# Decoder trunk with grouped experts, one core: expert gate and up weights laid out with eight consecutive rows per partition

## The reference, cut to what matters

```
def grouped_moe(x, w_router, b_router, w_gate, w_up, w_down):
    gates = shared_group_router(xt, w_router, b_router)      # two non-zero gates per token
    for e in range(N_EXPERTS):                               # 16
        h = silu(xt @ w_gate[e]) * (xt @ w_up[e])            # [512, 1024] @ [1024, 512], twice
        out = out + gates[:, e:e + 1] * (h @ w_down[e])      # [512, 512] @ [512, 1024]
```

## Time and profile before

| | |
|---|---|
| median of 3 runs | 888.58 us (884.96 to 889.7) |
| profiled execution | 889.47 us, span 888.0 us from first to last instruction |
| mean granted TensorE clock | 0.981 |
| PE busy, share of the span | 851.6 us, 96% |
| PEld | 707.0 us, 80% |
| DVE | 574.0 us, 65% |
| ACT | 465.0 us, 52% |
| POOL | 76.0 us, 9% |
| DMA | 195.87 MB in 168097 packets, mean 221 GB/s |

### The profile page before, as it was taken

The page is one execution under the profiler, slowest core; times in us unless marked ns, Lnnn a source line. Parts: engine busy times, 40 slices in busy tenths (PEclk is TensorE's granted clock), DMA queues, the critical chain, the costliest instruction groups (busy, mean ns, idle before and its releaser), DMA issues.

```text
span 888.0 us, 12634 instructions
## 1 busy us (share of the span) xinstructions
PE 851.6 (96%) x4090; PEld 707.0 (80%) x4091; DVE 574.0 (65%) x623; ACT 465.0 (52%) x482; POOL 76.0 (9%) x137
## 2 busy tenths in 40 slices
PE   9999999979999999999999999799999999999993
PEld 8788788858888888888888987688888888888751
DVE  4887444334448874423555698479898988888727
ACT  4555542423566653422325641477888787778610
POOL 1000000500000000000000002200101010010040
PEclk9999999989999999999999999799999999999997
DMA  7465555963333345433319915799999999999753
GB/s 203 171 182 165 173 191 193 256 239 91 95 94 95 95 114 170 119 100 112 95 52 325 293 41 214 262 338 379 380 372 382 382 381 371 380 381 382 245 185 122
DMA packets 168097, 195.87 MB, mean 221 GB/s; under 512 B 7998, under 2 KB 106918, under 8 KB 168070
## 3 DMA queue, kind: packets, MB, share of 16 engines
q1 hardware_dynamic: 154374, 157.69, 53.4%
q0 software_dynamic: 10624, 32.57, 10.7%
q10 hardware_dynamic: 3072, 5.24, 1.6%
HBM read 164.94 MB, written 30.54 MB: 220 GB/s over the span
## 4 chain that ended last, share of the span: by engine, by line
PE 72%; DMA 11%; DVE 9%; ACT 3%; issue 3%; POOL 1%; ACTq 0%; DVEq 0%; SPq 0%; POOLq 0%
PE psA L585 7%; PE psA L587 7%; PE psA L586 7%; DMA est<-in_w_exp_down_dram 6%; PE psB L585 6%; PE psB L587 6%; PE psB L586 6%; PE psA L756 4%; PE psA L758 4%; PE psA L757 4%; DVE elo L1334 2%; DMA wst<-in_w_out_dram 2%; PE psB L777 2%; PE psB L778 2%; PE psB L779 2%
## 5 line engine op out<-in xcount | busy, mean ns | idle before, releaser
L1334 DVE TENSOR_TENSOR elo<-est,ehi 128x2048 fp32r<-128x2048 f32 x94 | 211.5, 2288 | 37.3 <-ACT ehi L1005 32.0
L1005 ACT ACTIVATE ehi<-est 128x2048 fp32r<-128x2048 f32 x92 | 173.5, 1913 | 38.8 <-DMA est<-in_w_exp_down_dram 18.4
L1136 DVE TENSOR_TENSOR wlo<-wst,whi 128x1024 fp32r<-128x1024 f32 (+1 forms) x78 | 97.5, 1250 | 97.8 <-ACT whi L852 96.7
L852 ACT ACTIVATE whi<-wst 128x1024 fp32r<-128x1024 f32 (+1 forms) x78 | 83.9, 1076 | 92.5 <-PE psA L587 36.4
L756 PE MATMUL psA<-ehi,xe_hi 128*128 128x512 f32 x256 | 102.2, 399 | 1.9 <-DVE xe_lo L1527 1.8
L758 PE MATMUL psA<-ehi,xe_lo 128*128 128x512 f32 x256 | 100.5, 393 | 0.0
L757 PE MATMUL psA<-elo,xe_hi 128*128 128x512 f32 x256 | 100.5, 393 | 0.0
L585 PE MATMUL psB<-xT_hi,whi 128*128 128x512 f32 x208 | 80.9, 389 | 0.0
L586 PE MATMUL psB<-xT_lo,whi 128*128 128x512 f32 x208 | 80.9, 389 | 0.0
L587 PE MATMUL psB<-xT_hi,wlo 128*128 128x512 f32 x208 | 80.9, 389 | 0.0
L756 PEld LDWEIGHTS psA<-ehi,xe_hi 128*128 128x128 f32 x256 | 48.6, 190 | 12.8 <-DVE xe_lo L1527 3.1
(11 more groups left out here) (277 smaller groups left out, 1634.7 us busy)
## 6 DMA issues: line engine op xcount, KB each, us to landing
est<-in_w_exp_gate_dram SPq DMA_DIRECT2D x32, 1024.0 KB, 12.3
est<-in_w_exp_up_dram SPq DMA_DIRECT2D x32, 1024.0 KB, 10.8
est<-in_w_exp_down_dram SPq DMA_DIRECT2D x32, 1024.0 KB, 11.9
wst<-in_w_in_dram SPq DMA_DIRECT2D x60, 512.0 KB, 4.0
xs<-zero POOLq DMA_DIRECT2D x23, 512.0 KB, 2.9
wst<-in_w_out_dram SPq DMA_DIRECT2D x16, 512.0 KB, 6.4
wst<-in_w_branch_r_dram SPq DMA_DIRECT2D x8, 640.0 KB, 4.3
ys<-yb ACTq DMA_DIRECT2D x32, 160.0 KB, 5.1
```

What stands on the lines that cost most here:

```text
L852: A(whi[p][:, 0:K, :], wst[p][:, 0:K, :], ACT.Copy).then_inc(w_hi, 1)
L1005: A(ehi[s][:], est[s][:], ACT.Copy).then_inc(gu_hi if s < 4 else d_hi, 1)
L1136: V.tensor_tensor(wlo[p][:, 0:K, :], wst[p][:, 0:K, :], whi[p][:, 0:K, :], ALU.subtract).then_inc(w_lo, 1)
L1334: V.tensor_tensor(elo[s][:], est[s][:], ehi[s][:], ALU.subtract).then_inc(gu_lo if s < 4 else d_lo, 1)
```

## The change

Two things change together, in three lines.

- `load_expert` reads gate and up weights with the row index p*8 + k: partition p now holds the eight consecutive rows 8p to 8p+7, the first four in one piece and the last four in the other. So the part of a piece that goes to one partition is 8 KB without a gap in DRAM, and without a gap in the buffer. Down weights are loaded as before.
- The tokens' channels have to be grouped alike: piece k of the transpose is no longer columns 128k to 128k+127 of `xe` but every eighth column, k, k+8, k+16 and so on. Now the stationary operand of L744 and L788 is read with a step of 8 floats (32 bytes). What is written to PSUM, `xe_hi`, `xe_lo`, and all matmuls behind it keep their shapes, their number and their order. No instruction is added or removed, and no wait.

```
             if s < 4:
-                src = w.rearrange("(k p) n -> p k n", p=P)[:, 4 * (s % 2):4 * (s % 2) + 4, :]
+                src = w.rearrange("(p k) n -> p k n", p=P)[:, 4 * (s % 2):4 * (s % 2) + 4, :]
...
                 for k in range(KD):
                     mm = pe.transpose(psC[0][:, k // 4, (k % 4) * P:(k % 4 + 1) * P],
-                                      xe[:, k * P:(k + 1) * P], ident[:])
+                                      xe[:].rearrange("p (c k) -> p k c", k=KD)[:, k, :], ident[:])
...
                     mm = pe.matmul(psC[0][:, k // 4, (k % 4) * P:(k % 4 + 1) * P],
-                                   x1[:, t, k * P:(k + 1) * P], block0[:, t, :],
+                                   x1[:, t, :].rearrange("p (c k) -> p k c", k=KD)[:, k, :], block0[:, t, :],
                                    start=(t == 0), stop=(t == TT - 1))
```

## The result

Over 20 runs of each, the changed kernel takes 889.38 us (median) and the kernel before 886.66: the ratio is 1.0029, with a 95% interval of 1.0019 to 1.0040. It is slower by 0.3%, or 2.7 us, inside the 0.5% that I had called no change, and far from the 901.5 us that I held likeliest. The time lies in my range only because the range had been stretched to the free step.

A forecast was written before the change was run, and what follows sets the result against it. PE was taken to bound the expert stage, transfers right behind. 889.47 - 0.6 (loads) + 13.5 (strided operand: 11.5 + 2.0) = 902.4 us profiled, 901.5 as median; range 885.5 to 906, stretched to include the free step.

The forecast's parts named there:

- the free step: Rival: strided stationary loads in transposes and first block cost nothing, leaving only the loads' relief, 888.0 us median; chance 0.27.
- The packet line: Gate and up loads: 38 ns per KB plus 10 ns fixed per packet, so 8 KB pieces save 1.0 us per expert.
- What it brings the end: -0.6 us: Relieved loads: 0.4 us won at the last expert and 0.2 us in the output projection; bounds 0 to -1.5 us.
- `xe` lands 1.1 us later and stays covered: Expert stage: token rows queue behind longer packets, landing after 7.5 instead of 6.4 us, at no cost.
- The price of a strided load: 0.216 us instead of 0.109: TensorE's 128-column fp32 stationary loads in L744 and L788: a 32-byte step adds 0.107 us each.
- The road by VectorE's 1.84 ns an element: Price of a strided TensorE load taken from VectorE's 16-byte-step write: 0.236 us for 128 elements.
- What sets the pace of the transposes: `rows_t`: loading 128 fp32 weights sets the pace, so any slowing of the read is paid in full.
- The term of 11.5 us: Blocks 2 to 15: 14 times eight slower transpose loads in `rows_t`, 0.75 to 0.86 us per block.
- The first block: 2.0 us: L788's 64 strided loads add 6.8 us; after the covered wait and the clock, +1.2 to +2.8 us remain.
- the cover of 3.4 us: Before block 1: PE's wait for `xe` hides this much of L788's 6.8 us, so `rows_t(1)` starts 3.4 us later.
- the clock's gift: `gate_up(1)`: with a shorter wait before it, half clock need not follow, giving back up to 2.2 us.
- the two variants of the forecast, 1.2 and 2.8: First block's net cost: +1.2 us if half clock stays away behind it, +2.8 us if it returns; 2.0 taken.

The follow-up runs named there:

- e6: Kernel before with the eight transposes of `rows_t` replaced by plain fp32 products with the identity, no step: 898.43 us beside 885.11, one execution each.
- e7: Changed kernel with expert 0 in the old layout, L788 unstrided, and plain fp32 products reading `xe` at 32 bytes instead of the transposes: 927.07 us, one execution.
- e1: Kernel before with only the gate and up loads changed to 8 KB pieces, channels wrongly paired: 884.10 us, ratio 0.9977.
- e8: Repeat of e1, only the gate and up loads changed against the kernel before: 884.93 us against 886.80, ratio 0.9977.
- e3: Kernel before with only the transposes of `rows_t` reading `xe` at a step of 32 bytes: 887.31 us, ratio 1.0006.
- e5: Kernel before with extra rows of PE instructions at several steps and kinds in front of the first block: 939.07 us beside 885.11, one execution.
- e2: Kernel before with only L788 reading `x1` at a step of 32 bytes: 890.63 us, ratio 1.0050.
- e4: Changed kernel, but expert 0's gate and up weights keep the old layout and L788 has no step: 886.05 us, ratio 0.9997 to the kernel before.
- e9: Repeat of e4, the changed kernel with expert 0 in the old layout: 886.23 us, ratio 0.9992 to the kernel before.

## Why the prediction was wrong, point by point

- **PE bounds the expert stage, the transfers right behind.** Right. With the loads relieved, PE's period stayed at 17.69 to 17.73 us, and with PE lengthened (e6, e7) the time grew by what PE's rows grew, within the scatter of single executions.
- **The packet line.** Right in kind: the 8 KB pieces do go as long packets. The forecast was 32 x 30 ns = 1.0 us of transfer per expert in a cycle of 18.2, or 5.5%; the queue's price per MB fell by 5.7%.
- **What it brings the end: -0.6 us.** Too small. e1 and e8 measured -2.0 and -2.0 us (0.9977 both times; by the two intervals -0.5 to -3.6). The forecast's bounds were 0 and -1.5. In the traces I find the 0.4 us of the last expert. The wait for `xe` before block 1 is 2.6 us in e1 and e8 instead of 3.3, but e3 and e6, with the old loads, have 1.5 and 2.0, so it can't be put down to the loads. Which step gives the rest is not shown.
- **`xe` lands 1.1 us later and stays covered.** Right: 7.6 us instead of 6.4, and PE never waits for it.
- **The price of a strided load: 0.216 us instead of 0.109.** Right for a plain product, a little low: L788 went from 0.112 to 0.236, e5 shows 0.238. The road by VectorE's 1.84 ns an element gave 0.236.
- **What sets the pace of the transposes.** This is the step that failed. I compared the router's 16 moving columns with the transposes' 128, found 0.12 and 0.109 us, and concluded that both are paced by the load. But the router's are plain fp32 products and L744's are transposes. Equal paces were two different limits that happen to meet near 0.11 us. The weight load's own duration in the trace had the difference: 140 ns in L744, 192 in the plain products. I hadn't read it. Weight loads of L744 (PEld) from 600 to 820 us, the kernel before, then the one after:

```profile
L744 PEld LDWEIGHTS psC<-ident,xe 128*128 128x128 f32 x104 | 12.2, 140 | 1.7
```

```profile
L744 PEld LDWEIGHTS psC<-ident,xe 128*128 128x128 f32 x104 | 13.6, 192 | 1.0
```

  And the loads of L788, before and after (ns: least, median, most):

```profile
L788 PEld LDWEIGHTS psC<-block,x x64: 186/192/192, 543.5 to 550.5; 128*128 128x128 f32 x64
```

```profile
L788 PEld LDWEIGHTS psC<-block,x x64: 317/336/338, 541.8 to 556.8; 128*128 128x128 f32 x64
```

  The step does lengthen the transpose's load, by 52 ns, but only to the 192 ns that a plain product's load has without a step, and that one keeps a pace of 0.11 us. The pace of the transposes was 0.11 us at 140 ns already, so at a step of 1 something other than the load sets it, and a load of 192 ns still fits under that. That this is the moving pass fits all rows and is argued, not shown. The term of 11.5 us measured 14 x 0.02 = 0.3 us in the chain, and +0.5 us (-1.0 to +2.0) in e3. The period's 0.04 us more can't be laid to the step alone: it is 17.73 us in all four traces with strided transposes, but 17.73 in e1 as well, without them, and 17.69 in e8, which is the same kernel as e1.
- **The first block: 2.0 us.** The price was near (7.9 instead of 6.8 us), the cover of 3.4 us right for that trace, and what was wrong is the clock's gift. In the profiled execution of the kernel before, `gate_up(1)` ran at half clock (1.2 GHz) for 4.7 us. That of e2, whose L788 starts at 543.47 beside 543.50, had full clock from 560 us on, and its transposes of block 2 came only 1.3 us later (586.98 against 585.67). In that of the changed kernel half clock came back, and from the start of L788 to those transposes it took 44.8 us instead of 42.0, 2.8 more. These are the two variants of the forecast, 1.2 and 2.8, and for the one trace that I started from both are right. But over its runs e2 measured +4.4 us (3.0 to 5.9). The other traces say why. That same distance is 43.4 us in e2, and in the six traces with L788 unstrided and the transposes kept (before, e1, e3, e4, e8, e9) it is 37.3 to 42.0, with a mean of 39.9: the trace that I started from is the longest. The mean granted clock from 560 to 600 us was 0.87 in it, 0.91 in e1, e8 and e9, 0.96 in the changed kernel and 1.00 in e2, e3 and e4, so these traces don't show it to go by the step. It belonged to an execution that lay 2.8 us above its median, and I had booked what varies between executions as a saving. That 4.4 comes so near to 7.9 less 3.3 is partly luck too, since the wait for `xe` is 1.4 to 2.8 us in the traces of e1, e3, e4 and e6 to e9.
- **The anchor.** The 3 runs shown had a median of 888.58; 20 runs have 886.66. It moved the forecast by 1.9 us, small beside the 11.5.
- **The chances.** 0.27 for the step being free was too little for a price that no row showed. Twice as much doubt would have been fair, since I had an argument for it written down: a load uses half the rate that the moving operand reads at.

## What to carry to other kernels

Before a pace is put down to one half of an instruction pair, read the durations of both halves (weight load and matmul) for the very kind of instruction that is to change; two kinds with equal pace can have different limits. A layout that makes long DMA pieces at the price of a strided stationary operand is nearly free where that operand goes through a transpose, costs 8% where it faces 512 moving columns (0.246 us against 0.2275), and costs double at full clock where plain fp32 products with 16 or 128 columns read it, so find the one place of the second kind and leave it in the old layout. A saving that rests on where the clock fell in one trace is not booked before several runs show it.

## What the runs showed of the hardware that was not expected

- A load without a step follows the clock, a strided one doesn't. In e5 the clock stood at 0.50 from 566 to 586 us (third number from the right):

```profile
566.00:586.00 20.00, 20.00 (x80) 18.94 (x81) 0.00 (x0) 0.00 (x0) 0.00 (x0) 0.50 0.22 72
```

  There the loads of L798, without a step, took (570.20 - 566.79) / 16 = 0.213 us, twice the 0.107 of L796 at full clock, and those of L801 at 32 bytes (581.15 - 577.33) / 16 = 0.239, the same as the 0.238 of L795 at full clock. L798 and L801 read rounded fp32, L795 and L796 plain fp32. L788 has the same kind at both levels. How many of its matmuls fall in 2 us stands in brackets behind PE: in e3, without a step, 12 at mostly half clock and 21 at full clock,

```profile
547.00:549.00 2.00, 2.00 (x12) 2.00 (x12) 0.54 0.00 0
549.00:551.00 2.00, 2.00 (x21) 2.00 (x20) 1.00 0.15 59
```

  and in e2, with the step, 10 at either:

```profile
547.00:549.00 2.00, 2.00 (x10) 2.00 (x10) 0.50 0.00 0
...
553.00:555.00 2.00, 2.00 (x10) 2.00 (x10) 1.00 0.74 301
```

- The 0.239 / 128 = 1.87 ns per element is near what VectorE's strided write showed, 1.84. That the two have a common cause is not shown, and it is no price for every type: the bf16 loads at 16 bytes take 0.061 / 128 = 0.48 ns per element.
- The moving operand gets slower too: 0.46 us at a step of 16 bytes against 0.2275. The row at 8 bytes (L807) ran mostly at half clock and gives no price.
- Transposes at 8 and 16 bytes took 0.120 us, more than at 32 bytes (0.113). Their weight loads last longer as well, 209 and 212 ns against 193. No run explains it.
